# Gates of the second request: accumulating DMAs into a table in HBM instead of one-hot products, and gather turns dealt anew

## The reference

```python
v1, i1 = lax.top_k(s[:, :, 0], PEER_TOPK)
v2, i2 = lax.top_k(s[:, :, 1], PEER_TOPK)
cand = (v1[..., :, None] + v2[..., None, :]).reshape(t, PEER_HEADS, PEER_TOPK * PEER_TOPK)
cv, ci = lax.top_k(cand, PEER_TOPK)
e = (jnp.take_along_axis(i1, ci // PEER_TOPK, axis=-1) * PEER_NKEYS
     + jnp.take_along_axis(i2, ci % PEER_TOPK, axis=-1))
g = jax.nn.softmax(cv, axis=-1)
...
a = jnp.einsum('ckd,cd->ck', u_emb[ec], hc)
coef = (jax.nn.gelu(a.astype(jnp.float32), approximate=False) * gc).astype(v_emb.dtype)
return jnp.einsum('ck,ckd->cd', coef, v_emb[ec])
```

## Time and profile before

| | us |
|---|---|
| median of the three runs shown | 4191.82 |
| span of the profiled execution | 4193.2 |
| stretch: attention of the second request, 1280 to 1530 | 250 |
| top-k of the second request with 32 blocks of U, 2106 to 2407 | 301 |
| products of half 0, 2407 to 2596 | 189 |
| U 0 (32 blocks), 2596 to 2842 | 246 |
| V 0 (64 blocks), 2842 to 3207 | 365 |
| products of half 1, 3207 to 3326 | 119 |
| U 1 (64 blocks), 3326 to 3815 | 489 |
| V 1 (64 blocks), 3815 to 4193 | 378 |

### The profile page before, as it was taken

How to read it: one execution, slowest core, us unless ns; L and a number is a source line. 1 busy time by engine, 2 the same in 40 slices (tenths; PEclk the granted TensorE clock), 3 DMA queues, 4 the chain that set the end, 5 groups by cost and what they waited for, 6 DMA issues and landing times.

```text
span 4193.2 us, 60957 instructions
## 1 busy us (share of the span) xinstructions
PE 3546.2 (85%) x22046; PEld 3217.2 (77%) x22046; DVE 3103.5 (74%) x3905; ACT 1421.7 (34%) x1936; POOL 835.7 (20%) x772
## 2 busy tenths in 40 slices
PE   7997988852996338978888867999998999999998
PEld 6876987752775228976888857997887999998886
DVE  4654444468898777877789999887787777777786
ACT  4544433321443113333432201334442233333443
POOL 0000000000223543222111266222221012121221
PEclk9999998986998668989999956999998699999999
DMA  5651655532998888989877856998886188888887
GB/s 188 193 162 51 181 152 174 176 110 107 355 333 318 302 317 329 362 321 329 314 266 289 297 179 210 337 360 311 330 329 245 55 320 313 302 313 307 327 332 293
DMA packets 288251, 1099.78 MB, mean 262 GB/s; under 512 B 24832, under 2 KB 25216, under 8 KB 219008
## 3 DMA queue, kind: packets, MB, share of 16 engines
q1 hardware_dynamic: 208640, 528.55, 37.1%
q0 software_dynamic: 73728, 536.90, 33.8%
q10 hardware_dynamic: 5760, 32.80, 2.1%
HBM read 1087.67 MB, written 10.49 MB: 262 GB/s over the span
## 4 chain that ended last, share of the span: by engine, by line
PE 63%; DVE 14%; issue 11%; DMA 4%; POOL 4%; ACT 2%; DVEq 0%; ACTq 0%; PEldq 0%; POOLq 0%; PEld 0%; SPq 0%
PE ps L1083 17%; PE ps L1135 13%; PE ps L1307 13%; PE ps L1079 9%; PE ps L1280 5%; PE ps L1118 4%; POOL rows L305 3%; DVE rows L638 3%; DMA w<-v_emb 2%; DVE w_lo L655 2%; DVE pick L981 1%; DMA w<-w_out 1%; DVE w_lo L622 1%; ACT w_hi L327 1%; DMA gvec<-g_ffn_b 1%
## 5 line engine op out<-in xcount | busy, mean ns | idle before, releaser
L622 DVE TENSOR_TENSOR w_lo<-w,w_hi 128x1024 fp32r<-128x1024 f32 x752 | 918.9, 1224 | 642.4 <-ACT w_hi L327 589.9
L327 ACT ACTIVATE w_hi<-w 128x1024 fp32r<-128x1024 f32 x752 | 795.9, 1060 | 1244.6 <-PE ps L1083 375.3
L303 POOL TENSOR_TENSOR tick<-iota 128x1 f32<-128x1 f32 x256 | 167.8, 655 | 3201.0 <-DVE acc L642 1246.0
L638 DVE CUSTOM_DVE_ANT_0 rows<-rows,h 128x2048 f32<-128x2048 f32 x256 | 583.6, 2284 | 33.2 <-DMA rows<-u_emb,stage_i 31.2
L642 DVE SCALAR_TENSOR_TENSOR acc<-rows,stage_d,acc 128x2048 f32<-128x2048 f32 x256 | 600.3, 2345 | 6.5 <-DVE stage_d L633 5.4
L655 DVE TENSOR_TENSOR w_lo<-ps,w_hi 128x1024 fp32r<-128x1024 f32 x256 | 312.2, 1220 | 170.4 <-ACT w_hi L394 167.6
L394 ACT ACTIVATE w_hi<-ps 128x1024 fp32r<-128x1024 f32 x256 | 262.9, 1028 | 434.5 <-PE ps L1118 421.7
L305 POOL DMA_INDIRECT rows<-v_emb,stage_i x256 | 348.9, 1363 | 57.4 <-issue 39.3
L305 POOL DMA_INDIRECT rows<-u_emb,stage_i x256 | 318.8, 1246 | 57.7 <-issue 41.0
L1135 PE MATMUL ps<-ht_hi,w_lo 128*128 128x256 f32 x2048 | 292.3, 286 | 37.8 <-DVE w_lo L655 37.5
L1079 PE MATMUL ps<-w_lo,ht_hi 128*128 128x512 f32 x1024 | 281.3, 397 | 40.7 <-DVE w_lo L622 40.7
(11 more groups left out here) (180 smaller groups left out, 5157.5 us busy)
## 6 DMA issues: line engine op xcount, KB each, us to landing
w<-w_in SPq DMA_DIRECT2D x320, 512.0 KB
w<-u_emb SPq DMA_DIRECT2D x256, 512.0 KB
w<-v_emb SPq DMA_DIRECT2D x256, 512.0 KB
w<-w_out SPq DMA_DIRECT2D x64, 512.0 KB
w<-w_pq SPq DMA_DIRECT2D x64, 512.0 KB
w<-w_br_b SPq DMA_DIRECT2D x32, 512.0 KB
xin<-x ACTq DMA_DIRECT2D x4, 2048.0 KB, 8.9
w<-w_br_a SPq DMA_DIRECT2D x16, 512.0 KB
```

The lines of the kernel that those rows point to most:

```text
L327: act.activation(w_hi[:, j % 2, :, :], w[:, j % RING, :, :], ACT.Copy).then_inc(hi_ready, 1)
L622: dve.tensor_tensor(w_lo[:, j % 2, :, :], w[:, j % RING, :, :], w_hi[:, j % 2, :, :].bitcast(F32), ALU.subtract).then_inc(lo_ready, 1)
L638: dve.tensor_tensor_reduce(out=row, in0=row, in1=h2[0][:, t, :], scale=1.0, scalar=0.0, op0=ALU.mult, op1=ALU.add, accum_out=stage_d[:, j: ...
```

## The change

The one-hot products and all that belongs to them go. A table `grid` of 16384 x 256 floats (16.8 MB) lies in HBM, with one row of 256 tokens for each expert. POOL clears it at the start from a zeroed `rows` buffer with four DMAs of 4 MB. In the top-k DVE also works out the place of each pair (`spots` = 256 e + token), and POOL adds the gates there by indirect DMAs that accumulate, 128 single floats each: 128 such DMAs for each tile of 128 tokens. Before each new head it waits until the head before has landed (`scattered`). In V, SP loads the 128 KB of gates of a block (`load_gates`) into a ring of four ahead of the block's first slab, and DVE multiplies them into `coefs` (L1037 of the new file); V 0 begins to load once all gates have been added. `coefs` now holds the bare gelu.

The turns are dealt anew. U: 48 in the projection as before, 64 in attention, 32, 16, 16 and 16 as before, none in the top-k, and 64 in U 0. V: none in U 0, 64 in V 0, 128 in U 1, 64 in V 1.

```diff
+EXPERTS = NKEYS * NKEYS
+LATE_TURNS, V_TURNS, U_TURNS = 64, 64, 128
+LATE_GROUPS = LATE_TURNS // 8
+GRING = 4
...
+    grid = nc.dram_tensor("grid", (EXPERTS * TOK, 1), F32, kind="Internal").ap()
+    grid_rows = grid.rearrange("(b p t) o -> p b (t o)", p=P, t=TOK)
...
+            def load_gates(h, i, b):
+                sp.wait_ge(c_made, i * BODY + (HB * h + b + 1))
+                sp.dma_start(gates[:, b % GRING, :].unsqueeze(1),
+                             grid_rows[:, bass.ds(i * BODY + (HB * h + b), 1), :]).then_inc(gates_in[b % GRING], 16)
...
+                    if table and h == 0:
+                        for t in range(NT):
+                            sp.wait_ge(scattered[t], 16 * SEL)
...
         def _(pool):
+            pool.memset(rows[:, :, :], 0.0).then_inc(rows_zeroed, 1)
+            pool.wait_ge(rows_zeroed, 1)
+            for q in range(EXPERTS * TOK // (P * ROWS * D)):
+                pool.dma_start(grid_flat[q], rows[:, :, :].rearrange("p r d -> p (r d)")).then_inc(cleared, 16)
...
-            for table in range(2):
-                with pool.Fori(0, GROUPS) as i:
-                    for j in range(0, 8, 2):
-                        gather(i, j, table)
+            def scatter(t, c):
+                h = c // TOPK
+                if c % TOPK == 0 and h:
+                    pool.wait_ge(scattered[t], 16 * TOPK * h)
+                pool.indirect_dma_start(grid, bass.IndirectOffsetOnAxis(ap=spots[:, t, c:c + 1], axis=0),
+                                        gsel[1][:, t, c:c + 1], None, compute_op=ALU.add).then_inc(scattered[t], 16)
+            with pool.Fori(0, GROUPS - LATE_GROUPS) as i:
+                for j in range(0, 8, 2):
+                    gather(i, j, 0)
+            pool.wait_ge(spots_ready, 1)
+            for c in range(SEL):
+                scatter(0, c)
+            pool.wait_ge(spots_ready, 2)
+            per = SEL // (4 * LATE_GROUPS)
+            for i in range(LATE_GROUPS):
+                for j in range(0, 8, 2):
+                    gather(GROUPS - LATE_GROUPS + i, j, 0)
+                    for c in range(per):
+                        scatter(1, per * (4 * i + j // 2) + c)
+            with pool.Fori(0, GROUPS) as i:
+                for j in range(0, 8, 2):
+                    gather(i, j, 1)
...
                         if j % 2 == 0:
+                            act.wait_ge(c_made, i * BODY + (HB * h + j // 2 + 1 + GRING))
                             act.activation(c_hi[:, j // 2 % 2, :],
...
                     split_turned(table_g0[0][0] + j, j)
-                    if j % 4 != 3:
-                        turns(1, 1)
                     early_slabs[0] += 1
...
-                turns(r, 6)
+                turns(r, 2)
                 maxima(0)
...
-                    turns(r, 3 if u < 12 else 2)
+                    turns(r, 2)
...
+                    if r == 1:
+                        own.after(dve, dve.tensor_scalar(esum[:, :], esum[:, :], float(TOK), token[:, t:t + 1], ALU.mult, ALU.add))
+                        own.after(dve, dve.tensor_copy(spots[:, t, :], esum[:, :]))
...
+                if h == 0:
+                    pieces(HB - b0, 0, GROUPS - LATE_GROUPS, LATE_TURNS, (1, 1), u_slab)
+                    dve.wait_ge(copied, GROUPS + 1)
+                    dve.drain().then_inc(dots_done, 1)
+                else:
+                    pieces(HB, 1, V_TURNS // 8, U_TURNS, (0, 1), u_slab)
...
                 def v_slab(i, blocks, j):
+                    if j % 2 == 0:
+                        dve.wait_ge(gates_in[j // 2 % GRING], i * (16 * blocks // GRING) + 16 * (HB * h // GRING + j // 2 // GRING + 1))
+                        cb = coefs[:, bass.ds(i * blocks + j // 2, 1), :].rearrange("p a t -> p (a t)")
+                        dve.tensor_tensor(cb, cb, gates[:, j // 2 % GRING, :], ALU.mult).then_inc(c_made, 1)
                     split_lo(i * (2 * blocks) + (table_g0[h][1] + j), j)
...
-                        for m in range(8):
-                            for k in range(2):
-                                ins = pe.matmul(ps[:, c, m * HB:(m + 1) * HB], pick2[:, c, m, :], pick1[:, c, k, m, :],
-                                                start=(k == 0), stop=(k == 1))
-                        ins.then_inc(picks_free, 1)
```

More of the change, by code:

```diff
@@ L284, in _ @@
                         for j in range(2 * BODY):
+                            if table and j % 2 == 0:
+                                load_gates(h, i, j // 2)
                             sp.wait_ge(lo_ready, i * (2 * BODY) + (table_g0[h][table] + j - RING + 1))
@@ L678, in stream @@
             def stream(ph, r):
-                k0 = taken[0] // 8
-                with dve.Fori(0, ph["pairs"]) as i:
-                    for j in range(2 * SPC):
-                        split_lo(i * (2 * SPC) + (ph["g0"] + j), j)
-                        if r == 1 and j % 2:
-                            turn(i + k0, j // 2, 0, 8 * k0 // SEL)
-                if r == 1:
-                    taken[0] += 8 * ph["pairs"]
+                k0, count = taken[0] // 8, 8 * ph["pairs"]
+                if r == 1 and 8 * k0 // SEL != (8 * k0 + count - 1) // SEL:
+                    for i in range(2 * SPC * ph["pairs"]):
+                        split_lo(ph["g0"] + i, i)
+                        turns(1, i % 2)
+                else:
+                    with dve.Fori(0, ph["pairs"]) as i:
+                        for j in range(2 * SPC):
+                            split_lo(i * (2 * SPC) + (ph["g0"] + j), j)
+                            if r == 1 and j % 2:
+                                turn(i + k0, j // 2, 0, 8 * k0 // SEL)
+                    if r == 1:
+                        taken[0] += count
             def inverse_root(own, mean, root, out, tmp):
@@ L949, in _, with pieces, piece, u_slab @@
                     own.after(dve, dve.tensor_tensor(gv, gv, gsum[:, :].unsqueeze(2).to_broadcast([P, PH, TOPK]), ALU.mult))
-                if r == 1:
-                    dve.drain().then_inc(sel_ready, 1)
-                else:
+                    if r == 1:
+                        dve.drain().then_inc(spots_ready, 1)
+                if r == 0:
                     dve.tensor_copy(stage_i[:, :], eidx[:, 0:8]).then_inc(staged, 1)
                 leave(dve, "dve"); n += 1
-            assert taken[0] == NT * SEL
-            dve.wait_ge(copied, GROUPS + 1)
-            dve.drain().then_inc(dots_done, 1)
+            assert taken[0] == NT * SEL - LATE_TURNS
             for h in range(HALVES):
+                def pieces(count, table, K0, n_turns, tiles, slab):
+                    rounds = len(tiles)
+                    per, per_turns = 2 * count // rounds, n_turns // rounds
+                    def piece(i, tile):
+                        k = 0
+                        for j in range(per):
+                            slab(i, per // 2, j)
+                            while k < (j + 1) * per_turns // per:
+                                turn(i * (per_turns // 8) + (K0 + k // 8), k % 8, table, tile)
+                                k += 1
+                    if len(set(tiles)) == 1:
+                        with dve.Fori(0, rounds) as i:
+                            piece(i, tiles[0])
+                    else:
+                        for i, tile in enumerate(tiles):
+                            piece(i, tile)
+                enter(dve, "dve", n)
+                b0 = 0 if h else EARLY
+                def u_slab(i, blocks, j):
+                    split_turned(i * (2 * blocks) + (table_g0[h][0] + 2 * b0 + j), j)
+                if h == 0:
+                    pieces(HB - b0, 0, GROUPS - LATE_GROUPS, LATE_TURNS, (1, 1), u_slab)
+                    dve.wait_ge(copied, GROUPS + 1)
+                    dve.drain().then_inc(dots_done, 1)
+                else:
+                    pieces(HB, 1, V_TURNS // 8, U_TURNS, (0, 1), u_slab)
+                leave(dve, "dve"); n += 1
                 enter(dve, "dve", n)
@@ L1003, in _ @@
-                leave(dve, "dve"); n += 1
-                def table(K0, rounds, count, n_turns, slab):
-                    per, per_turns = 2 * count // rounds, n_turns // rounds
-                    with dve.Fori(0, rounds) as i:
-                        k = 0
-                        for j in range(per):
-                            slab(i, per // 2, j)
-                            while k < (j + 1) * per_turns // per:
-                                turn(i * (per_turns // 8) + (K0 + k // 8), k % 8, 1, h)
-                                k += 1
@@ L1061, in _ @@
             pe.sem_inc(acc_free, 2)
-            for sem in (picks_free, spread, weighed, a_free, c_made):
-                pe.sem_inc(sem, 2)
+            pe.sem_inc(a_free, 2)
             def slab(g_, j, ks, form, lhs, b0, first, last):
```

139 lines of the change are left out of this document (33 added, 106 removed).

## The result

The change made the kernel slower, by little: 4211.02 us (median of 10 runs, 4197.36 to 4217.62) against 4192.69 us for the kernel before in the same comparison (10 runs), a ratio of 1.0043 with a 95% interval of 1.0032 to 1.0055. The forecast was 4085 us and faster. The profiled execution has a span of 4215.7 us, against 4193.2.

The account below looks back on a forecast made before the run. PE was taken to bound most of 4193.2 us, except products, top-k and the second attention. Savings of 74 us before 2407 and 35 after gave 4084, forecast 4085; own range 4010 to 4170, whole range 3980 to 4330.

Parts of the forecast that it names:

- change 4's price, p = 1.4 us: POOL's time per accumulating scatter, taken from the gather, with ends 1.25 and 2.83 us; it made U 0 400 us.
- 39 + 256p: Length of U 0 in us when POOL is the bound, with p the price of one scatter.
- the first wait: DVE's wait at U 0's first late gather, behind tile 0's scatters on POOL's queue: some 77 us.
- 21 us for waits at heads: POOL's 7 waits of 3 us each for a head's scatters to land, among tile 0's scatters.
- the rival: Dear scatter: a scatter between U's late gathers costs twice the assumed price or more; slower from p = 1.84; chance 0.27.
- 35 us of waits at tile 1's heads: Seven more POOL waits in U 0, now behind gathers, at 5 us each.
- Change 3's 15 us: Clearing the 16.8 MB table at the start, beside other loads: 15 us more, between 0 and 44.
- 45 and 44: Us saved in the second request's attention and top-k as turns leave them; PE is late next in the top-k.
- V 0 and V 1: Stretches with more turns, DMA late before PE: 404 us against 365 before, and 412 against 378.
- the gates' fetch, 40 us: Loading 8.4 MB of gates in 1 KB pieces during V 0, taken between 29 and 58 us.
- 380 GB/s: Rate assumed for full DMA engines, from ten-microsecond stretches with mean 384; it made U 1 535 us.
- the other rivals: DMA does not bind: U 1 stays 489 us, 3966 total, chance 0.10; poor use at 341 GB/s: 4234 us, chance 0.11.

Follow-up runs that it names:

- e7: Changed kernel with clearing in the first request's attention and all 64 late turns in the first half of the second request's top-k; 4127.08 us, ratio 0.9835.
- e2: Changed kernel with scatters that write instead of adding; 4077.75 us, ratio 0.9731 to the kernel before.
- e1: Changed kernel with only the clearing moved from the start into the first request's attention; 4173.41 us, ratio 0.9958 to the kernel before.
- e9: Changed kernel with late clearing, gates of equal experts summed first on DVE, and scatters that only write; 4079.29 us, ratio 0.9727.
- e10: Changed kernel with late clearing, gates summed first on DVE, writing scatters, and 32 of 64 late turns moved into the top-k; 4029.30 us, ratio 0.9614.
- e3: Changed kernel without any of the 256 scatters or the wait for them; 3907.55 us, ratio 0.9319 to the kernel before.
- e4: Changed kernel with 64 of tile 0's scatters ahead and the other 64 dealt among the late gathers' steps; 4216.57 us, ratio 1.0057.

## Why the prediction was wrong

**The step that failed is change 4's price, p = 1.4 us.** It was taken from the gather, as "the nearest row", with the gather's price as the lower end. The runs show that the lower end was the price of a scatter that writes (0.97 + 0.30), and that adding costs 0.58 us more on POOL, with four and a half times the packets. In the prediction's own formula, 39 + 256p, p = 1.855 makes 514 us in place of 400; the first wait that it gives, 128 x 1.855 + 21 - 124 = 134 us, was measured as 139.2 (of its 21 us for waits at heads, 14.0 came). I had weighed "accumulating must read before it writes" as a reason for the rival, and set against it that gathers of the same number of pieces are cheap; that second argument counted pieces of memory, while the price hangs on what is done with them. The rival named p = 1.84 as the point from which the kernel is slower. The measured pitch lies 0.015 us beyond. That the kernel came out so near to no change is chance all the same, for the other terms moved too, by +18, -12 and -27 us and by what follows.

**The second part of the same step: nothing was charged for POOL beside DVE's turns.** Of the 548 us, 34 are not in the formula even with the right p. The formula hides more: it has 35 us of waits at tile 1's heads, and 0.4 us came. Without them, 32 mixed steps of 3.35 + 4 x 1.855 us are 345 us, and the mixed part lasted 410. POOL's scatters and ticks (the `tick` ahead of two gathers, 0.35 us in the formula) in it:

```profile
L333 POOL DMA_INDIRECT grid<-gsel,spots x129 | 262.2, 2033 | 39.4 <-issue 39.0 <-DMA grid<-gsel,spots 0.4
...
L323 POOL TENSOR_TENSOR tick<-iota 128x1 f32<-128x1 f32 x32 | 46.9, 1466 | 0.0
```

POOL's order of time in 30 us of the mixed part after:

```profile
2608.95 1.62 POOL L333 DMA_INDIRECT grid<-gsel,spots  x1 [0.30 <-issue]
...
2612.76 2.88 POOL L333 DMA_INDIRECT grid<-gsel,spots  x1 [0.31 <-issue]
2615.94 1.55 POOL L333 DMA_INDIRECT grid<-gsel,spots  x1 [0.30 <-issue]
...
2625.10 3.35 POOL L333 DMA_INDIRECT grid<-gsel,spots  x1 [0.30 <-issue]
```

DVE's in the same 30 us:

```profile
2611.91 2.29 DVE L663 CUSTOM_DVE_ANT_0 rows<-rows,h 128x2048 f32<-128x2048 f32 x1 [4.51 <-DMA rows<-u_emb,stage_i]
...
2614.13 1.22 DVE L680 TENSOR_TENSOR w_lo<-ps,w_hi 128x1024 fp32r<-128x1024 f32 x1
2616.24 2.29 DVE L663 CUSTOM_DVE_ANT_0 rows<-rows,h 128x2048 f32<-128x2048 f32 x1 [0.89 <-DMA rows<-u_emb,stage_i]
...
2624.73 2.29 DVE L663 CUSTOM_DVE_ANT_0 rows<-rows,h 128x2048 f32<-128x2048 f32 x1 [5.05 <-DMA rows<-u_emb,stage_i]
...
2626.95 1.22 DVE L680 TENSOR_TENSOR w_lo<-ps,w_hi 128x1024 fp32r<-128x1024 f32 x1
```

The scatter of 2612.76 meets a turn that began at 2611.91. DVE's next instruction begins at 2614.13, and the scatter ends at 2615.64, 1.51 us later (1.44 after the turn's own end); the one of 2625.10 ends at 2628.45, 1.50 us after DVE's next at 2626.95. Both look as if they had begun only when the turn was over. The scatter of 2615.94, which the turn of 2616.24 found already begun, took its 1.55. In e7, where U's splits run without turns, 118 scatters took 1.55 us each. What e7 took out of U 0 were turns and their gathers together, and no run has the gathers alone, but the trace of the kernel after parts the two. Of its 256 scatters, 44 took 2.0 us or more and all others 1.62 at most. Each of the 44 began while DVE ran an operation with two inputs of 128 x 2048 floats, and ended 1.42 to 1.45 us after that operation's end. For 39 it was a turn; for five it was a step of the top-k (`cand`, L944, or `eq`, L962 and L966), while no gather was under way. One of these, POOL's row and DVE's:

```profile
2297.66 3.25 POOL L333 DMA_INDIRECT grid<-gsel,spots  x1 [0.30 <-issue]
...
2297.19 2.29 DVE L962 TENSOR_TENSOR eq<-cpf,iota 128x2048 f32<-128x2048 f32 x1
```

Scatters that began beside U's splits, beside the maxima, or beside the sum of L969 over 128 x 2048 floats with one input, were not held up. So it is the turn on DVE, and not its gather. In e2, where scatters write, 36 are long in the same way and end 0.84 to 0.88 us after the operation. In e1, e2, e9 and e10 seven scatters were not held up by such an operation; each began within 0.04 us of its start. The Trainium skill (GPSIMD Engine Reference, Specifications) has POOL's way into SBUF shared with DVE, with contention where a DVE instruction has two SBUF inputs. This trace agrees: the turn has two (`rows` and `h2`), and so have `cand` and `eq`, while the split of U has one, since it reads the other from PSUM. The row that could have warned me was among those I read: the gather's mean of 2.53 us beside the products' DVE work.

**Change 3's 15 us** were 39 at the first slab. I had asked whether there was room for the bytes beside the slabs of `w`, and found it: the slabs lost nothing that shows, for the first request's projection of q, k and v took PE 267 us, 270 before. But POOL's writes meet the constants at the very start, on which the first normalisation waits, before any stretch that I had looked at. The size was inside my bounds (0 to 44), the mechanism of its lower end was not the one that decides. e1 shows that the 37.6 us depend on the place alone.

**What was right.** Attention and top-k fell by 57 and 46 us for 45 and 44, and in the top-k PE is what is late next, as said. V 0 and V 1 were missed by 8 us and 1 us. That does not show the price of the gates' fetch, 40 us: no run leaves it out, and it stands in a sum with a rate, 380 GB/s, that was too low for U 1. V 0 also holds some 21 us that the sum has no term for, from 2884 to 2905, in which the last scatter lands (10.3 us) and then the first slab of V (10.6 us). That the DMA engines bind U 1 was right, at 399 GB/s rather than 380, 27 us better. Both of the other rivals fall with this: U 1 moved more than 341 GB/s, and it did not come down to 489 us. The 358 GB/s that the Trainium skill (DMA: Bandwidth & Descriptors, Specifications) gives for a core were no ceiling here either: 399 GB/s over 508 us. The Trainium skill's rule on pieces below 512 B, on the same page, would have the adding scatters slow on the DMA engines; alone with them, from 2336 to 2474 us, the engines were at a share of 0.22 for 4 GB/s. That is dear for so few bytes, but POOL was what was full, busy for 106 of 138 us with 0.30 us to each next scatter. The ends that the prediction gives for U 0, 362 and 765, are 359 and 763 by its own formula; nothing hangs on that.

**Why slower and not faster.** Neither miss would have done it alone. With the clearing elsewhere the same scatters give 4173 us (e1); with writing scatters the same clearing gives 4078 us (e2). Both are faster than before. The 308 us of products are gone, and the scatters cost 303 us in their place (e3): they stand on POOL's queue, and DVE, and behind it PE, wait for the rows that come after them there.

## To carry to other kernels

When work is moved onto an engine that was idle, add up its whole queue from the moment the work can start to the moment it is needed: 256 scatters of 1.855 us and 64 gathers made POOL the bound of a stretch in which it had been 26% busy, and the other order of e4 did not help. An operation that no row shows is not priced by its nearest neighbour when it does something more at the far end; where the break-even price lies 0.4 us above the guess, that is most of the forecast. When work is moved the other way, onto an engine that has gaps, its price is its full time less the gaps (e7: 64 turns of 2.36 us, 37 us of gaps, 113 us). And a large transfer "in the background" cost 39 us where the program starts and everybody waits for small constants, and nothing that could be seen where the DMA engines stood still (e1).

## What the hardware showed

- An indirect DMA of 128 single floats takes 1.55 us on POOL when it adds, in 144 packets, and 0.97 us when it writes, in 32 packets; a gather of 128 rows of 8 KB takes 0.95 us.
- A scatter that POOL begins while DVE runs an operation over two SBUF inputs of 128 x 2048 floats (2.29 us) ends 1.42 to 1.45 us after that operation (44 of 44 in the kernel after; the longest took 3.66 us). Beside an equally long sum over one such input it takes its 1.55.
- Beside four SBUF-to-HBM writes of 4 MB at the start, the `iota` (64 KB) on ACT's queue landed after 54.5 us and not 15.5, while slabs of `w` on SP's queue landed after 7.6 us in the same stretch.
- Over the 508 us of U 1 the DMA engines moved 399 GB/s, with this one core in the profile.
